# The first sixteen modulation chunks: products and row-block sums on VectorE, TensorE sums over the partitions alone

## The chip, the cores and the metric
The kernel runs on one core of a Trainium2 chip. The metric is the device time of one execution in microseconds; lower is better. TensorE is called PE in the profile, VectorE DVE, ScalarE ACT, GpSimd POOL, SyncE SP.

## The reference, cut to what matters
A stack of two transformer-like layers (gated linear attention, attention, convolution, feed-forward) is run on a context and a latent sequence of 256 tokens each, 1024 channels wide, and then a second stack of two layers. Everything is float32. Each layer of the first stack begins with a modulation, of which the first layer's first two parts, shift and scale, are needed before any other matrix product:

```python
silu_c = jax.nn.silu(c)            # (1, 1024), the latent's condition
silu_cc = jax.nn.silu(c_ctx)       # (1024,), the context's
mod = (silu_c @ w_ada[l] + b_ada[l])[:, None, :]       # w_ada[l]: 1024 x 6144
sh1, sc1, g1, sh2, sc2, g2 = jnp.split(mod, 6, axis=-1)
mod_c = jnp.split(silu_cc @ w_ada[l][:, :n_cm * D_MODEL] + ..., n_cm)
hc = _layernorm(xc) * (1.0 + mod_c[1]) + mod_c[0]
```

Shift and scale are columns 0 to 2047 of `w_ada[0]`: 16 chunks of 128 columns, each a sum over 1024 rows (8 row blocks of 128), for two condition vectors (streams).

## The kernel before, in words
Activations lie with channels on the partitions: `X[:, c, t]` is channel block c of 8, token t. Each large product is made of three float32r products (high and low parts of weights and activations). The weights come as one stream of tiles through three slots: SP loads a slot, ScalarE rounds it to the high part (L1040, `split_to`), GpSimd subtracts for the low part (L1009), PE multiplies (L472 to L474; L485 to L489 for the first two chunks of a pass).

The head of the program goes as follows. SP (L409 to L422) issues loads in this order on one queue: the condition vectors `cvec`, the context tokens `X`, `const1`, then sixteen loads of 512 KB, one per modulation chunk, into `a_first` (eleven places in the arena, five in `s_f32`, L288), then the first three tiles of the stream, then the parameters (`vec1`, the low-rank weights `wglr`, the masks as float32 in `stage`, the latent tokens). ScalarE applies SiLU to `cvec` (L1351), splits the three stream tiles (L1353), then serves the layer norm: a table load, squares (L1077), and the root of the variance (L1069). PE sums the tokens over the channels (L564), then the squares (L573), by products with the constant matrix `mean1024`. VectorE centres the tokens (`centre`, L1588) and turns the root into 1/std (`inverse`, L1577 to L1580).

Then comes `first_modulation` on each engine, between `inverse` and the scaling of the centred tokens. PE runs `ada` for the 16 chunks of `FIRST_UNITS` (L509 to L523): for each of 8 row blocks a product with the 128 x 128 weight block as the stationary operand and the two columns of `cvec` as the moving one, accumulated in a PSUM bank. ScalarE copies each chunk's two columns from PSUM to `mod` (L1234). VectorE casts the masks to bytes (L1908), adds the bias in two instructions of 8 chunks (L1769, `modulation`), waits for ScalarE's rounding of `wglr` (L1361) and subtracts for its low part (L1913). After that VectorE scales each chunk of tokens (`scale_chunk`, L1592), ScalarE adds the shift and rounds it (L1084), VectorE makes its low part (L1599), and PE begins with the dense products, which wait for both.

Order between engines is by semaphores that only count up. `lin_done` and `lin_evac` count PSUM banks filled and emptied, four banks in turn. `step` on VectorE makes it wait for its own last instruction. The other 80 modulation chunks (`ADA_LATER`) are loaded one at a time by ScalarE into `a_raw` and run in gaps later on; their work isn't changed. `gate_buf` and `y_buf` are buffers of 512 columns each that later stages use for sigmoids and branch outputs; they are unused in the head.

Of the kernel before, what the change touches and what calls it, by code (L numbers as in the profile page):

```python
# [28 lines left out]
P = 128  # L29
D = 1024  # L30
KC = D // P
S = 256
# [97 lines left out]
FIRST_UNITS = [("ada", (0, c)) for c in range(ADA_FIRST)]  # L130

# [64 lines left out]
def program(nc, stream, ada_in, xt_in, cvec_in, vec1_in, vec2_in, glr_in, a2_in, const1_in, const2_in, small2_in, mask_in, out):  # L196
# [5 lines left out]
    with ExitStack() as ctx:  # L202
# [85 lines left out]
        a_first = [view(arena, 4 * S * c, KC, P) for c in (*range(10), 12)]  # L288
        a_first += [s_f32[:, 4 * c:4 * c + 4, :].rearrange("p a (b m) -> p (a b) m", m=P) for c in range(5)]
# [25 lines left out]

        def c1(name):
            at, n = CONST1[name]
            return const1[:, at:at + n]
# [9 lines left out]
        def v2(l, name, c=0):  # L328
# [7 lines left out]
        first_landed = [sem(f"first_landed{i}") for i in range(4)]  # L336
# [5 lines left out]
                 "params", "c_landed", "ada_landed", "x_landed", "b2_landed", "stored",  # L342
# [65 lines left out]
        def _(sp):  # L408
# [4 lines left out]
            for c in range(ADA_FIRST):  # L413
                sp.dma_start(a_first[c], ada_in[c]).then_inc(first_landed[c // 4], 16)
# [21 lines left out]
        def _(pe):  # L436
# [70 lines left out]
            ada_done = {}  # L507

            def ada(unit):  # L509

                k0 = len(ada_done)
                ada_done[unit] = k0
                if k0 < ADA_FIRST:
                    w = a_first[k0]
                    if k0 % 4 == 0:
                        pe.wait_ge(first_landed[k0 // 4], 4 * 16)
                else:
                    w = a_raw
                    pe.wait_ge(sems["ada_landed"], 16 * (k0 - ADA_FIRST + 1))
                o = bank()  # L520
                for k in range(KC):
                    mm = pe.matmul(o[:, 0:2], w[:, k, :], cvec[:, k, :], start=k == 0, stop=k == KC - 1)  # L522
                done(mm)  # L523

# [249 lines left out]
            for turn, (l, s) in enumerate(PASSES):  # L774
# [249 lines left out]
        def _(act):  # L1024
# [208 lines left out]
            def ada(l, c):  # L1233
                moved(act.activation(mod[:, l, c, :], arrived(0)[:, 0:2], ACT.Copy))  # L1234
                ada_moved.append((l, c))
                following = len(ada_moved) - ADA_FIRST
                if 0 < following < len(ADA_LATER):
                    act.dma_start(a_raw[:, :, :], ada_in[ADA_FIRST + following]).then_inc(sems["ada_landed"], 16)
# [1112 lines left out]
```

## Time and profile before

| | us |
|---|---|
| median of 3 runs (lowest to highest) | 3371.79 (3366.3 to 3377.26) |
| the profiled execution, its own time | 3385.26 |
| its span in the profile | 3383.5 |
| mean granted TensorE clock | 0.928 of full |
| PE busy | 3011.1 (89%) |
| DVE busy | 2166.1 (64%) |
| POOL busy | 2127.6 (63%) |
| ACT busy | 1521.1 (45%) |

The profiled execution is one run with the recorder on; its own time stands beside its span, and both lie above the median of the three runs. Durations are read from it. Lines such as L522 are lines of the kernel before. PEclk is the clock that TensorE was granted, as a share of 2.4 GHz. A float32 product on PE is recorded as two matmuls and two weight loads.

### The profile page before, as it was taken

What the parts mean: (1) busy time and instruction counts of PE and PEld (TensorE: products, weight loads), DVE (VectorE), ACT (ScalarE), POOL (GpSimd) and SP (SyncE); (2) the same over time, 40 slices, a digit from 0 to 9 for tenths busy, and PEclk for the clock granted to TensorE, in tenths of its full rate; (3) what the DMA queues carried; (4) which work ended last, traced back from release to release, by engine and by line L of the source; (5) the groups of instructions that cost most, each with busy time, mean ns of one, the idle gap of its engine ahead of it and who ended that gap; (6) DMA issues with size and microseconds to landing.
All of it is one profiled execution on the core that took longest, in us unless ns stands there. A gap on an engine that the chain in (4) does not pass through costs nothing.

```text
span 3383.5 us, 59733 instructions
## 1 busy us (share of the span) xinstructions
PE 3011.1 (89%) x21908; PEld 2837.3 (84%) x21908; DVE 2166.1 (64%) x2956; ACT 1521.1 (45%) x3134; POOL 2127.6 (63%) x1906
## 2 busy tenths in 40 slices
PE   6879988889987999889988889888899989998998
PEld 5879887889987977889987789678799869996998
DVE  0776475677695569567654965785676566646655
ACT  1443434344554433435555534334444445554544
POOL 0784545648887453656865964537487637873677
PEclk6889988999998989989999999889899989998999
DMA  5334333435433333334532443223455314542454
GB/s 200 104 127 138 113 112 103 144 116 177 165 125 126 118 106 116 122 113 148 175 131 81 132 144 119 94 82 110 143 179 171 119 46 160 175 156 67 134 169 166
DMA packets 121589, 441.84 MB, mean 131 GB/s; under 512 B 13552, under 2 KB 15600, under 8 KB 120992
## 3 DMA queue, kind: packets, MB, share of 16 engines
q1 hardware_dynamic: 109568, 393.35, 34.8%
q10 hardware_dynamic: 11808, 45.42, 3.9%
q8 instruction: 162, 2.65, 0.3%
q14 instruction: 51, 0.42, 0.0%
HBM read 437.67 MB, written 1.05 MB: 130 GB/s over the span
## 4 chain that ended last, share of the span: by engine, by line
issue 36%; POOL 33%; PE 21%; DVE 7%; ACT 2%; POOLq 1%; DMA 0%; DVEq 0%; ACTq 0%; SPq 0%
POOL w_lo L1009 33%; PE lin L472 5%; PE lin L473 5%; PE lin L474 5%; DVE arena L1702 4%; PE aux L710 2%; PE lin L522 1%; ACT w_hi L1040 1%; DVE s_lo L1640 1%; PE aux L598 1%; POOLq L1011 0%; ACT arena L1200 0%; PE lin L730 0%; POOLq L1007 0%; DVE small L1716 0%
## 5 line engine op out<-in xcount | busy, mean ns | idle before, releaser
L1009 POOL TENSOR_TENSOR w_lo<-w_raw,w_hi 128x256 fp32r<-128x256 f32 (+1 forms) x1902 | 2127.4, 1147 | 1249.5 <-ACT w_hi L1040 1246.7
L472 PE MATMUL lin<-h_hi,w_hi 128*128 128x256 f32 x3584 | 1043.0, 291 | 53.0 <-POOL w_lo L1009 33.6
L473 PE MATMUL lin<-h_lo,w_hi 128*128 128x256 f32 x3584 | 1025.3, 286 | 0.0
L474 PE MATMUL lin<-h_hi,w_lo 128*128 128x256 f32 x3584 | 1024.2, 286 | 0.0
L1040 ACT ACTIVATE w_hi<-w_raw 128x512 fp32r<-128x512 f32 x1446 | 827.8, 623 | 159.6 <-PE lin L472 106.7
L472 PEld LDWEIGHTS lin<-h_hi,w_hi 128*128 128x128 f32 x3584 | 700.0, 195 | 71.2 <-issue 40.2
L473 PEld LDWEIGHTS lin<-h_lo,w_hi 128*128 128x128 f32 x3584 | 699.9, 195 | 0.4
L474 PEld LDWEIGHTS lin<-h_hi,w_lo 128*128 128x128 f32 x3584 | 699.0, 195 | 0.0
L1702 DVE SCALAR_TENSOR_TENSOR arena<-arena,vec 128x256 f32<-128x256 f32 x720 | 453.2, 701 | 0.1
L472 PE MATMUL lin<-s_hi,w_hi 128*128 128x256 f32 x1392 | 415.7, 299 | 31.1 <-DVE s_lo L1640 26.3
L473 PE MATMUL lin<-s_lo,w_hi 128*128 128x256 f32 x1392 | 404.0, 290 | 0.0
L474 PE MATMUL lin<-s_hi,w_lo 128*128 128x256 f32 x1392 | 403.2, 290 | 0.0
L472 PEld LDWEIGHTS lin<-s_hi,w_hi 128*128 128x128 f32 x1392 | 277.1, 199 | 46.5 <-DVE s_lo L1640 34.3
L473 PEld LDWEIGHTS lin<-s_lo,w_hi 128*128 128x128 f32 x1392 | 278.1, 200 | 1.1 <-issue 0.8
L474 PEld LDWEIGHTS lin<-s_hi,w_lo 128*128 128x128 f32 x1392 | 277.5, 199 | 0.0
L1678 DVE TENSOR_TENSOR y_buf<-gate_buf,y_buf 128x256 f32<-128x256 f32 x110 | 147.2, 1338 | 182.7 <-ACT y_buf L1173 182.7
L1640 DVE TENSOR_TENSOR s_lo<-y_buf,s_hi 128x256 fp32r<-128x256 f32 x110 | 232.6, 2115 | 3.8
L1577 DVE RECIPROCAL rstd<-std 128x256 f32<-128x256 f32 (+1 forms) x34 | 59.5, 1749 | 247.9 <-ACT std L1069 247.9
L1657 DVE SCALAR_TENSOR_TENSOR X<-X,gate_buf 128x256 f32<-128x256 f32 x72 | 76.7, 1066 | 149.2 <-ACT gate_buf L1181 70.1
L522 PEld LDWEIGHTS lin<-cvec,a_raw 128*128 128x128 f32 x1280 | 160.1, 202 | 14.3 <-DMA a_raw<-in_ada 11.9
L522 PE MATMUL lin<-cvec,a_raw 128*128 128x2 f32 x1280 | 157.5, 254 | 9.9 <-DMA a_raw<-in_ada 9.9
L500 PE MATMUL lin<-w_hi,h_hi 128*128 128x256 f32 x320 | 97.4, 304 | 54.2 <-POOL w_lo L1009 53.9
(251 smaller groups left out, 4384.7 us busy)
## 6 DMA issues: line engine op xcount, KB each, us to landing
w_raw<-in_stream SPq DMA_DIRECT2D x723, 512.0 KB, 3.3
a_raw<-in_ada ACTq DMA_DIRECT2D x80, 512.0 KB, 3.4
arena<-in_ada SPq DMA_DIRECT2D x11, 512.0 KB, 12.5
s_f<-in_ada SPq DMA_DIRECT2D x5, 512.0 KB, 15.8
X<-in_tokens SPq DMA_DIRECT2D x2, 1024.0 KB, 12.1
arena<-in_const ACTq DMA_DIRECT2D x1, 1856.0 KB, 9.5
arena<-in_small ACTq DMA_DIRECT2D x1, 1536.0 KB, 12.9
out<-arena SPq DMA_DIRECT2D x1, 1024.0 KB, 3.9
```

Source lines behind the costliest of these rows:

```text
L472: used(pe.matmul(o, whi, hi[:, k, :], start=k == 0, stop=False), first)
L473: pe.matmul(o, whi, lo[:, k, :], start=False, stop=False)
L474: mm = pe.matmul(o, wlo, hi[:, k, :], start=False, stop=k == kcs - 1)
L500: mm = pe.matmul(o[:, 0:2 * P], xhi, whi, start=k == 0, stop=False)
L522: mm = pe.matmul(o[:, 0:2], w[:, k, :], cvec[:, k, :], start=k == 0, stop=k == KC - 1)
L710: mm = pe.matmul(pair[kt][:, h * P:(h + 1) * P], part, part, start=True, stop=True)
L1009: ins = pool.tensor_tensor(w_lo[:, slot, part], w_raw[:, slot, part], w_hi[:, slot, part].bitcast(F32), ALU.subtract)
L1040: act.activation(w_hi[:, slot, part], w_raw[:, slot, part], ACT.Copy).then_inc(sems["hi_ready"], 1)
L1640: dve.tensor_tensor(lo, y, hi.bitcast(F32), ALU.subtract).then_inc(sems[name], 1)
L1657: dve.scalar_tensor_tensor(x[:, c, :], x[:, c, :], alpha, gate_buf[:, c % 2, :], ALU.mult, ALU.add).then_inc(sems["r_ready"], 1)
L1678: step(dve.tensor_tensor(y, gate_buf[:, c % 2, :], y, ALU.mult))
L1702: dve.scalar_tensor_tensor(CV[:, c, :], YP[:, c, tap:tap + S], v1(l, "conv_w", c * TAPS + tap), CV[:, c, :], ALU.mult, ALU.add).then_inc(s ...
```

## The change
The weights of the first 16 chunks are laid out in device memory as one array `first` of 128 partitions x 8 row blocks x 2048 columns, and loaded in five groups of 4, 4, 4, 2 and 2 chunks. For each group and each of the two streams VectorE multiplies the eight row blocks by the condition's values (a column of scalars per row block) and adds them up, into `gate_buf` for the context stream and `y_buf` for the latent one: one product and seven multiply-adds per stream. PE then takes each chunk's 128 x 128 part of such a sum as the stationary operand and one column of `mean1024` (1/1024) as the moving one, so that it sums over the partitions; ScalarE multiplies by 1024 while it copies the group's columns to `mod`. VectorE waits for that copy before it begins the next group. The mask cast moves behind the groups and the bias.

```diff
+FIRST_GROUPS = [(0, 4), (4, 4), (8, 4), (12, 2), (14, 2)]
...
-        a_first = [view(arena, 4 * S * c, KC, P) for c in (*range(10), 12)]
-        a_first += [s_f32[:, 4 * c:4 * c + 4, :].rearrange("p a (b m) -> p (a b) m", m=P) for c in range(5)]
+        a_first = [view(arena, 0, KC, 4 * P), view(arena, 16 * S, KC, 4 * P),
+                   s_f32[:, 0:16, :].rearrange("p (k a) m -> p k (a m)", k=KC),
+                   view(arena, 32 * S, KC, 2 * P), view(arena, 48 * S, KC, 2 * P)]
...
+        first_parts = [t[:, :, :].rearrange("p a b -> p (a b)") for t in (gate_buf, y_buf)]
...
 SP:
-            for c in range(ADA_FIRST):
-                sp.dma_start(a_first[c], ada_in[c]).then_inc(first_landed[c // 4], 16)
+            for g, (c, k) in enumerate(FIRST_GROUPS):
+                sp.dma_start(a_first[g], first_in[:, :, c * P:(c + k) * P]).then_inc(first_landed[g], 16)
...
 PE:
+            def first_sums():
+                for g, (_, k) in enumerate(FIRST_GROUPS):
+                    pe.wait_ge(sems["part_ready"], 2 * g + 2)
+                    o = bank()
+                    for c in range(k):
+                        for st, part in enumerate(first_parts):
+                            at_col = 2 * c + st
+                            mm = pe.matmul(o[:, at_col:at_col + 1], part[:, c * P:(c + 1) * P], c1("mean1024")[:, 0:1],
+                                           start=True, stop=True)
+                    done(mm)
...
                         layernorm(x)
+                        first_sums()
                         pe.wait_ge(sems["c_ready"], at.up("c_ready"))
-                        for u in FIRST_UNITS:
-                            unit(l, s, u)
...
 ACT:
             def first_modulation():
-                for u in FIRST_UNITS:
-                    unit(0, u)
+                for c, k in FIRST_GROUPS:
+                    moved(act.activation(mod[:, 0, c:c + k, :], arrived(0)[:, 0:2 * k].rearrange("p (c s) -> p c s", s=2), ACT.Copy,
+                                         scale=float(D)))
...
 DVE:
             def first_modulation():
+                dve.wait_ge(sems["c_ready"], 1)
+                for g, (c, k) in enumerate(FIRST_GROUPS):
+                    dve.wait_ge(first_landed[g], 16)
+                    if g:
+                        dve.wait_ge(sems["lin_evac"], n.at("lin_evac"))
+                    for kc in range(KC):
+                        for st, part in enumerate(first_parts):
+                            w, by = a_first[g][:, kc, :], cvec[:, kc, st:st + 1]
+                            if kc == 0:
+                                ins = dve.tensor_scalar(part[:, 0:k * P], w, by, None, ALU.mult)
+                            else:
+                                dve.wait_ge(sems["dve_step"], n.at("dve_step") - (1 if kc < KC - 1 or st == 0 else 0))
+                                ins = dve.scalar_tensor_tensor(part[:, 0:k * P], w, by, part[:, 0:k * P], ALU.mult, ALU.add)
+                            if kc < KC - 1:
+                                ins.then_inc(sems["dve_step"], 1)
+                                n.up("dve_step")
+                            else:
+                                ins.then_inc(sems["part_ready"], 1)
+                    n.up("lin_evac")
+                    pending.extend((0, c + i, n.at("lin_evac")) for i in range(k))
                 dve.wait_ge(sems["params"], PARAMS)
+                modulation()
                 step(dve.tensor_copy(masks[:, :, :], stage[:, :, :]))
-                for u in FIRST_UNITS:
-                    unit(0, u)
-                modulation()
```

The rest of the diff keeps the count of the other 80 chunks' loads, which no longer follow 16 others in the same array.

## Rows read from the trace of the kernel before

**Rows 1.** The page: busy time of the engines; the loads of X.
```profile
PE 3011.1 (89%) x21908; PEld 2837.3 (84%) x21908; DVE 2166.1 (64%) x2956; ACT 1521.1 (45%) x3134; POOL 2127.6 (63%) x1906
...
X<-in_tokens SPq DMA_DIRECT2D x2, 1024.0 KB, 12.1
```

**Rows 2.** Who waited for whom, 0 to 105 us: total, times, longest (us).
```profile
ACT mod L1234 <- PE lin L522: 49.5, 16, 3.2
DVE mod L1769 <- ACT mod L1234: 47.8, 2, 27.1
```

**Rows 3.** Timeline of the head: start, length (us), engine, line, operation, count, idle before.
```profile
16.90 2.48 DVE L1588 TENSOR_TENSOR arena<-X,aux 128x512 f32<-128x512 f32 x4 [16.90 <-PE aux L564]
...
35.16 1.15 ACT L1040 ACTIVATE w_hi<-w_raw 128x512 fp32r<-128x512 f32 x2 [0.15 <-DMA w_raw<-in_stream]
...
38.40 5.97 PE L573 MATMUL aux<-M,const 128*128 128x256 f32 x16 [21.54 <-ACT M L1077]
...
44.21 35.53 PE L522 MATMUL lin<-cvec,arena 128*128 128x2 f32 x176
...
44.82 1.75 DVE L1577 RECIPROCAL rstd<-std 128x256 f32<-128x256 f32 x1 [25.45 <-ACT std L1069]
...
46.61 0.42 DVE L1578 SCALAR_TENSOR_TENSOR tmp<-aux,rstd 128x256 f32<-128x256 f32 x1
...
47.53 0.42 DVE L1580 SCALAR_TENSOR_TENSOR rstd<-tmp,rstd 128x256 f32<-128x256 f32 x1
47.99 1.16 DVE L1908 CAST masks<-arena 128x1920 uint8<-128x1920 f32 x1
...
79.60 17.21 PE L522 MATMUL lin<-cvec,s_f 128*128 128x2 f32 x80
...
96.84 0.17 ACT L1234 ACTIVATE mod<-lin 128x2 f32<-128x2 f32 x1 [3.24 <-PE lin L522]
...
97.12 0.18 DVE L1769 SCALAR_TENSOR_TENSOR mod<-mod,vec 128x16 f32<-128x16 f32 x1 [27.13 <-ACT mod L1234]
97.85 0.96 DVE L1913 TENSOR_TENSOR wglr_lo<-arena,wglr_hi 128x768 fp32r<-128x768 f32 x1 [0.56 <-ACT wglr_hi L1361]
98.72 0.87 DVE L1592 SCALAR_TENSOR_TENSOR arena<-arena,mod,rstd 128x256 f32<-128x256 f32 x2
```

**Rows 4.** Stretches of the head: length, busy time per engine, PEclk, DMA share, GB/s.
```profile
6.00:8.00 2.00, 0.00 (x0) 0.00 (x0) 0.00 (x0) 0.00 (x0) 0.00 (x0) 1.00 1.07 421
20.00:24.00 4.00, 0.00 (x0) 0.00 (x0) 0.00 (x0) 0.00 (x0) 0.00 (x0) 0.50 1.03 410
38.00:42.00 4.00, 3.60 (x9) 2.89 (x10) 0.00 (x0) 1.90 (x4) 3.55 (x6) 0.50 1.02 347
48.00:97.00 49.00, 48.81 (x229) 48.72 (x229) 1.32 (x2) 2.57 (x16) 0.00 (x0) 0.50 0.00 1
100.00:104.00 4.00, 3.45 (x16) 3.48 (x17) 4.00 (x11) 2.32 (x6) 0.00 (x0) 0.50 0.00 0
104.00:108.00 4.00, 4.00 (x34) 4.00 (x34) 1.76 (x6) 0.96 (x3) 0.00 (x0) 0.95 0.02 4
```

**Rows 5.** Timeline, VectorE and PE at the start of the dense work.
```profile
99.78 0.48 DVE L1599 SCALAR_TENSOR_TENSOR h_lo<-arena,mod,h_hi 128x256 fp32r<-128x256 f32 x1 [0.18 <-ACT h_hi L1084]
...
100.52 0.29 PEld L485 LDWEIGHTS lin<-h_hi,w_hi 128*128 128x128 f32 x1 [3.80 <-issue]
...
100.97 0.48 DVE L1592 SCALAR_TENSOR_TENSOR arena<-arena,mod,rstd 128x256 f32<-128x256 f32 x1
```

**Rows 6.** Lengths of one instruction (ns, min/median/max): L1807 and L1588.
```profile
L1807 DVE SCALAR_TENSOR_TENSOR arena<-arena x8: 1212/1451/1687, 204.8 to 1950.7; 128x1024 f32<-128x1024 f32 x8
...
L1588 DVE TENSOR_TENSOR arena<-X,aux x52: 673/681/689, 16.9 to 2648.2; 128x512 f32<-128x512 f32 x52
```

**Rows 7.** L522: lengths in the head (ns), and one chunk later in the kernel.
```profile
L522 PEld LDWEIGHTS lin<-cvec,s_f x80: 333/333/333, 79.5 to 96.4; 128*128 128x128 f32 x80
...
236.69 1.84 PE L522 MATMUL lin<-cvec,a_raw 128*128 128x2 f32 x16
```

More of the change, by code:

```diff
@@ L193, with program @@
 assert sorted(u[1] for u in FIRST_UNITS + ADA_LATER) == [(l, c) for l in range(DEPTH) for c in range(ADA_CHUNKS)]
-def program(nc, stream, ada_in, xt_in, cvec_in, vec1_in, vec2_in, glr_in, a2_in, const1_in, const2_in, small2_in, mask_in, out):
+def program(nc, stream, first_in, ada_in, xt_in, cvec_in, vec1_in, vec2_in, glr_in, a2_in, const1_in, const2_in, small2_in, mask_in, out):
     F32 = mybir.dt.float32
@@ L335, in program @@
         landed = [sem(f"landed{i}") for i in range(SLOTS)]
-        first_landed = [sem(f"first_landed{i}") for i in range(4)]
+        first_landed = [sem(f"first_landed{i}") for i in range(len(FIRST_GROUPS))]
         NAMES = ("hi_ready",
@@ L505, in token_major @@
                             done(mm)
-            ada_done = {}
+            ada_done = []
             def ada(unit):
[L511 to L519, printed above, removed]
+                ada_done.append(unit)
+                pe.wait_ge(sems["ada_landed"], 16 * len(ada_done))
                 o = bank()
                 for k in range(KC):
-                    mm = pe.matmul(o[:, 0:2], w[:, k, :], cvec[:, k, :], start=k == 0, stop=k == KC - 1)
+                    mm = pe.matmul(o[:, 0:2], a_raw[:, k, :], cvec[:, k, :], start=k == 0, stop=k == KC - 1)
                 done(mm)
+            def first_sums():
[8 more added lines that the diff above has]
+                    done(mm)
             def unit(l, s, u):
@@ L1235, in ada @@
                 ada_moved.append((l, c))
-                following = len(ada_moved) - ADA_FIRST
-                if 0 < following < len(ADA_LATER):
-                    act.dma_start(a_raw[:, :, :], ada_in[ADA_FIRST + following]).then_inc(sems["ada_landed"], 16)
+                if len(ada_moved) < len(ADA_LATER):
+                    act.dma_start(a_raw[:, :, :], ada_in[len(ada_moved)]).then_inc(sems["ada_landed"], 16)
             def unit(l, u):
@@ L2187, in ada_tiles @@
     both = [tiles(w["w_ada"]).reshape(ADA_CHUNKS, KC, P, P).transpose(0, 2, 1, 3) for w in layers]
-    return np.stack([both[l][c] for _, (l, c) in FIRST_UNITS + ADA_LATER])
+    return np.stack([both[l][c] for _, (l, c) in ADA_LATER])
 def half_tiles(gate, up, down):
@@ L2331 @@
         "stream": np.concatenate(stream).reshape(LOADS, TILES, P, P).transpose(0, 2, 1, 3).reshape(LOADS, P, TILES * P),
+        "first": layers[0]["w_ada"][:, 0:ADA_FIRST * P].reshape(KC, P, ADA_FIRST * P).transpose(1, 0, 2),
         "ada": ada_tiles(layers),
```

4 lines of the change are left out of this document (2 added, 2 removed).

## Prediction, written before the changed kernel was run

> **What bounds the kernel now.** The page first: TensorE (PE) is busy for 89% of the span, but that is an average over stages, and the change touches only the head of the program [rows 1]. So the next view is who waited for whom in the head: ScalarE waits 49.5 us for the modulation's matmuls (L522), and VectorE 47.8 us for ScalarE behind them; no wait is longer in total [rows 2]. The timeline of that stretch gives the order [rows 3]. The weight loads land; ScalarE, which waited for the last of them, splits until 36.31; PE sums ScalarE's squares from 38.40 to 44.37; after ScalarE's root VectorE makes 1/std, 44.82 to 47.95. Beside that PE begins the 16 chunks at 44.21 and ends them at 96.81. Then ScalarE moves the last chunk (96.84 to 97.01), VectorE adds the bias (97.12 to 97.30), splits the low-rank weights (97.85) and starts to scale chunks at 98.72; PE's dense work begins at 100.52 [rows 5]. POOL is idle, all slots being full [rows 4]. Nothing runs in the gap that could absorb a delay, so a microsecond here is one at the end.
>
> **What goes.** 16 chunks of 8 products, each recorded as two matmuls: 256 records from 44.21 to 96.81, 52.6 us, 0.2055 each on average, 0.2135 in the steady part at 3.416 per chunk (ScalarE waits 3.24 and works 0.17 for each) [rows 3]. The granted clock there is 0.50, so this is the 1.2 GHz level [rows 4]. PE could start them at 44.2, beside VectorE's 1/std; the new work stands behind 1/std in VectorE's own order and starts at 47.99, where the mask cast stands now. So to gain anything it would have to be done in under 49.1 us (97.12 less 47.99).
>
> **What comes: VectorE's sums.** Per group 8 row blocks by 2 streams, 16 instructions: 2 plain products and 14 multiply-adds. Three groups are 512 columns wide, two 256: 42 and 28 multiply-adds, 6 and 4 products. No row shows a multiply-add of 512 columns. The nearest in kind are L1592 and L1599, a column of scalars as here, 256 columns: 0.48 long, but started every 0.40 (99.78 to 100.97 is three steps) with a semaphore wait between them [rows 5]. The new ones wait for the instruction before the last, so they can follow one another as closely. For the width: 1024 columns take 1.212 at best [rows 6] against 0.42 for 256 (L1578 [rows 3]), 1.03 ns a column; 256 more add 0.265, so 0.66 apart. Bounds: 0.60 (four subtractions of 512 columns, 0.681 each, in 2.48 [rows 3, 6]) and 0.73 (each waits for the one before: L1578 to L1580 are two steps in 0.92 at 256 columns, plus 0.265 each). The products take one tensor: the cast's 1.16 for 1920 columns is 0.60 ns a column, so I take 0.40 and 0.27. Sum: 42 x 0.66 + 6 x 0.40 + 28 x 0.40 + 4 x 0.27 = 27.7 + 2.4 + 11.2 + 1.1 = **42.4 us**. With 0.60 and 0.36 it is 38.8, with 0.73 and 0.46 it is 47.1. POOL is idle throughout, so nothing contends with VectorE for SBUF but PE's reads, which I cost at nothing; L1807's span from 1.212 to 1.687 [rows 6] shows what company can cost, and the high bound stands for it.
>
> The rows give 0.40 for 256 columns. The Trainium skill, "VectorE: DVE Perf Modes", section "Side-by-side: where the cycles go for N=2048 bf16", counts columns + 8 + about 150 cycles at 0.96 GHz, an estimate of 0.70 for 512 and 0.43 for 256. By that the sum would be about 45 us and the time 3 us longer; the rows at 256 speak for less, and I keep them.
>
> **The new wait.** There is one pair of partial sums (gate_buf, y_buf). From the second group on, VectorE waits until ScalarE has moved the previous group, so each group is a serial round trip: VectorE's last end is 0.09 behind its issue pace; PE's start behind VectorE 0.26 (L1599 ends at 100.26, PE's weight load starts at 100.52 [rows 5]); the matmuls; ScalarE 0.03 later, 0.17 long; VectorE 0.11 later [rows 3]. A matmul with one column instead of two still loads 128 x 128 weights (0.333 long each, overlapped [rows 7]); I take nothing for the column saved, so 8 products for a group of four chunks cost as much as one chunk did: 16 x 0.2135 = 3.42, plus 0.23 to fill and drain the first and last. That is 4.3 per wide group, 2.6 per narrow one: 3 x 4.3 + 2 x 2.6 = **18.1 us**, of which nothing is covered, because VectorE has no other work and the next group's first product writes the same buffer. PE's clock: idle from 16.9 it was granted 0.50, and it stayed at 0.50 through narrow matmuls [rows 4], so the bursts run slow. At full clock they would be worth half: 16 records in 1.84 [rows 7].
>
> **The end of the head.** Start 47.99 + 42.4 + 18.1 = 108.5 where 97.12 stands now: +11.4. Both bias additions of 0.18 now stand at the end; one was hidden before (L1769 waited twice, 20.7 and 27.1 [rows 2]): +0.2. The mask cast of 1.16 was hidden under PE and now lies behind them, in front of the split of the low-rank weights, but it covers the 0.56 that VectorE waited for ScalarE there [rows 3]: net +0.7. Sum **+12.3 us**.
>
> **The loads.** 8.39 MB as before. Five issues instead of 16 take SP out of the way sooner, worth nothing: the engines are full at 410 GB/s from 6 us on, the queue is served in order and the stream's tiles stand behind the same bytes. The runs shrink from 4 KB to 2 KB and 1 KB. X has 1 KB runs (256 columns), and the stretch that carries it shows 421 [rows 1, 4]; so I take nothing for it. The other bound is the 347 GB/s of 38 to 42 us: 24.2 us instead of 20.5, +3.7. All have landed before the stream's tiles, by 36, long before VectorE asks at 48.
>
> After the head all is as before, moved; the banks' order shifts by 11 chunks, nobody waits for that. The granted clock rises about 4 us after dense work starts, as now (0.50 in 100 to 104 us, 0.95 in 104 to 108 [rows 4]); at half clock those 4 us hold 2 us of work, so a rise that comes at once or twice as late is worth 2 us either way.
>
> **Rivals.** (a) *Full clock or quicker hand-over in the bursts:* 1.8 less three times, 0.9 twice, 7.2 off: +5.1, 3377, no measurable change. For it: PE was at 1.00 while idle at 6 to 8 us [rows 4]. Against: 0.50 in the idle stretch of 20 to 24 us. 0.15. The low bound for VectorE (-3.6) gives +8.7, which also can't be told from zero. (b) *VectorE serial, or the loads late:* 47.1 instead of 42.4 is +17.0; late loads move the root and all behind it by 3.7, +16.0; both, +20.7, 3392. For it: a wait stands before every instruction and the rows' runs are new. 0.15. (c) *Not slower:* VectorE forms two columns a cycle in the multiply-add as in the cast. Then 48 x 0.40 + 32 x 0.27 = 27.8 replaces 42.4: -14.6, so -2.3, 3369. It decides at about 0.40 apart for 512 columns. Against: the multiply-adds of 256 and 1024 columns differ by 1.03 ns a column, where the cast shows 0.60. 0.04. (d) *The change doesn't do what it says:* PE isn't relieved, since a narrow matmul costs its weight load. That is in the forecast: PE still does 32 products of 128, in a place where VectorE stands still for them.
>
> **Numbers.** A measurement of this kernel tells 0.3%, 10.1 us, from no change. The profiled execution took 3385.3 (span 3383.5) against a median of 3371.8 (3366.3 to 3377.3); the sum is a difference and goes on either: 3397.6 profiled, 3384.1 for the median. Forecast 0.66; its own band of +8 to +16 lies for about a quarter on the near side of +10.1. Slower: 0.66 x 0.74 + 0.15 = 0.64. Faster: 0.03, half of (c) and some disturbance. Same: 0.33. The range goes from (a) to (b) with 2 us for the median's scatter: 3375 to 3393.
>
> **What would show it.** VectorE busy for some 42 us in about 48 to 111 us, in five blocks of about 10.2 and 6.2 with four gaps of 4.3 and 2.6; PE in five bursts, three of 16 records and two of 8, 0.21 apart, clock 0.50; modulation at 108.5, mask cast behind it, PE's first dense work at 112.8. Wrong if the 512-column instructions start under 0.60 apart, the gaps are under 3 us, or 1/std ends elsewhere than at 48.

## The result, and the profile after

| | us |
|---|---|
| kernel before, median of 4 runs | 3374.53 (3366.3 to 3382.57) |
| changed kernel, median of 4 runs | 3404.72 (3402.06 to 3407.11) |
| ratio | 1.0089, 95% interval 1.0062 to 1.0116 |
| forecast | 3384.1, range 3375 to 3393: +12.3 |
| profiled execution of the changed kernel | 3405.85 (before: 3385.26) |
| its span | 3404.1 (before: 3383.5) |
| its mean granted clock | 0.925 (before: 0.928) |

Slower, as forecast, but by 30 us instead of 12. The two spans are 20.6 us apart.

The page of the changed kernel, the rows that answer to [rows 1]: PE works 34 us less (the 128 products that go took 52.6, 32 new ones come), VectorE 38 us more.

```profile
PE 2977.3 (87%) x21716; PEld 2803.1 (82%) x21716; DVE 2204.3 (65%) x3036; ACT 1518.5 (45%) x3123; POOL 2122.4 (62%) x1906
...
arena<-in_first SPq DMA_DIRECT2D x2, 2048.0 KB, 16.4
```

Who waited for whom, 0 to 115 us (total, times, longest), against [rows 2]: PE now waits for VectorE, ScalarE for PE, and VectorE four times for ScalarE, 14.1 us in total.

```profile
ACT mod L1366 <- PE lin L530: 61.5, 5, 17.0
...
PE lin L530 <- DVE y_buf L1927: 48.1, 5, 13.8
...
DVE gate_buf L1924 <- ACT mod L1366: 14.1, 4, 4.0
```

Timeline of its head, against [rows 3, 5], first VectorE, then PE and ScalarE.

```profile
47.75 1.75 DVE L1585 RECIPROCAL rstd<-std 128x256 f32<-128x256 f32 x1 [28.12 <-ACT std L1077]
...
50.91 0.49 DVE L1924 TENSOR_SCALAR gate_buf<-arena,cvec 128x512 f32<-128x512 f32 x1
51.32 0.48 DVE L1924 TENSOR_SCALAR y_buf<-arena,cvec 128x512 f32<-128x512 f32 x1
51.71 0.75 DVE L1927 SCALAR_TENSOR_TENSOR gate_buf<-arena,cvec,gate_buf 128x512 f32<-128x512 f32 x1
52.38 0.75 DVE L1927 SCALAR_TENSOR_TENSOR y_buf<-arena,cvec,y_buf 128x512 f32<-128x512 f32 x1
53.04 0.75 DVE L1927 SCALAR_TENSOR_TENSOR gate_buf<-arena,cvec,gate_buf 128x512 f32<-128x512 f32 x1
...
65.02 0.49 DVE L1924 TENSOR_SCALAR gate_buf<-arena,cvec 128x512 f32<-128x512 f32 x1 [3.95 <-ACT mod L1366]
...
93.95 0.48 DVE L1927 SCALAR_TENSOR_TENSOR gate_buf<-arena,cvec,gate_buf 128x256 f32<-128x256 f32 x1
94.34 0.48 DVE L1927 SCALAR_TENSOR_TENSOR y_buf<-arena,cvec,y_buf 128x256 f32<-128x256 f32 x1
...
110.20 0.17 DVE L1777 SCALAR_TENSOR_TENSOR mod<-mod,vec 128x16 f32<-128x16 f32 x1 [2.15 <-ACT mod L1366]
110.41 1.16 DVE L1937 CAST masks<-arena 128x1920 uint8<-128x1920 f32 x1
111.60 0.96 DVE L1939 TENSOR_TENSOR wglr_lo<-arena,wglr_hi 128x768 fp32r<-128x768 f32 x1
112.48 0.88 DVE L1600 SCALAR_TENSOR_TENSOR arena<-arena,mod,rstd 128x256 f32<-128x256 f32 x2
```

```profile
40.54 6.76 PE L582 MATMUL aux<-M,const 128*128 128x256 f32 x16 [23.43 <-ACT M L1085]
61.13 0.59 PE L530 MATMUL lin<-const,gate_buf 128*128 128x1 f32 x2 [13.83 <-DVE y_buf L1927]
...
114.28 0.55 PE L489 MATMUL lin<-h_hi,w_hi 128*128 128x256 f32 x1 [4.38 <-DVE h_lo L1607]
```

```profile
34.73 3.72 ACT L1048 ACTIVATE w_hi<-w_raw 128x512 fp32r<-128x512 f32 x6 [31.96 <-DMA w_raw<-in_stream]
...
64.74 0.18 ACT L1366 ACTIVATE mod<-lin 128x8 f32<-128x8 f32 x1 [17.02 <-PE lin L530]
```

The multiply-adds of 512 columns start 0.66 apart, those of 256 0.39 to 0.40. VectorE stands idle for 3.95 before a group of four. The first token chunk is scaled at 112.48 instead of 98.72: the head is 13.8 us longer. That leaves 6.8 of the trace's 20.6 us for the 3290 us behind the head.

Stretches of the head (columns as in [rows 4]; the last is GB/s). The loads are slower than the 410 of [rows 4] from 20 us on:

```profile
20.00:24.00 4.00, 0.00 (x0) 0.00 (x0) 0.00 (x0) 0.00 (x0) 0.00 (x0) 0.50 1.05 387
24.00:28.00 4.00, 0.00 (x0) 0.00 (x0) 0.00 (x0) 0.00 (x0) 0.00 (x0) 0.50 1.07 371
28.00:32.00 4.00, 0.00 (x0) 0.00 (x0) 0.00 (x0) 0.00 (x0) 0.00 (x0) 0.50 1.11 352
```

### The profile page after: what moved, and what is told of

The parts are those of the page before. It is cut to its first block, busy times and chain, and to the rows that moved or that the text cites. A ratio compares the mean times of both kernels' runs of the same rounds, so it can differ in the third digit from the quotient of the medians.

```text
span 3404.1 us, 59409 instructions
## 1 busy us (share of the span) xinstructions
PE 2977.3 (87%) x21716; PEld 2803.1 (82%) x21716; DVE 2204.3 (65%) x3036; ACT 1518.5 (45%) x3123; POOL 2122.4 (62%) x1906
## 3 DMA queue, kind: packets, MB, share of 16 engines
q8 instruction: 169, 2.77, 0.4%
## 4 chain that ended last, share of the span: by engine, by line
issue 30%; PE 29%; POOL 28%; DVE 10%; ACT 2%; POOLq 1%; DMA 1%; DVEq 0%; ACTq 0%; SPq 0%
POOL w_lo L1017 28%; PE lin L476 7%; PE lin L477 6%; PE lin L478 6%; DVE arena L1710 5%; PE aux L719 2%; PE lin L519 2%; DVE s_lo L1648 1%; PE aux L607 1%; ACT w_hi L1048 1%; PE lin L739 1%; PE aux L647 1%; ACT arena L1208 1%; DVE small L1724 1%; DVE s_hi L1647 0%
## 5 line engine op out<-in xcount | busy, mean ns | idle before, releaser
L1648 DVE TENSOR_TENSOR s_lo<-y_buf,s_hi 128x256 fp32r<-128x256 f32 x110 | 221.9, 2017 | 4.0 <-DVE s_hi L1647 0.3
L519 PEld LDWEIGHTS lin<-cvec,a_raw 128*128 128x128 f32 x1280 | 158.3, 200 | 13.6 <-DMA a_raw<-in_ada 11.1
L504 PE MATMUL lin<-w_hi,h_hi 128*128 128x256 f32 x320 | 96.8, 303 | 53.1 <-POOL w_lo L1017 52.6
## 6 DMA issues: line engine op xcount, KB each, us to landing
X<-in_tokens SPq DMA_DIRECT2D x2, 1024.0 KB, 11.1
s_f<-in_first SPq DMA_DIRECT2D x1, 2048.0 KB, 20.9
```

The lines of the kernel that those rows point to most:

```text
L504: mm = pe.matmul(o[:, 0:2 * P], xhi, whi, start=k == 0, stop=False)
L519: mm = pe.matmul(o[:, 0:2], a_raw[:, k, :], cvec[:, k, :], start=k == 0, stop=k == KC - 1)
L1648: dve.tensor_tensor(lo, y, hi.bitcast(F32), ALU.subtract).then_inc(sems[name], 1)
```

## The experiments

Where a text below speaks of microseconds "to the median", it is the ratio less one, times the median of the kernel before in the same comparison. "Head" is the start of the first scaled token chunk against the 98.72 of the first trace of before.

Two readings stood against each other at first: that a microsecond of head costs more than one at the end, and that the change also costs something behind the head, where its code does nothing.

### Is it the head, and which part of it?

**after_again** is the changed kernel once more.

> The changed kernel once more, beside the kernel before in five rounds. Its trace showed the head 13.8 us longer (the first scaling of tokens at 112.48 instead of 98.72), its span 20.6 and the medians 30. If the head is all there is, the ratio settles at +14 us (1.004) and the rest was scatter of the few runs. If something behind the head costs too, it stays at +25 to +35 us.

1.0085 (1.0059 to 1.0112), +28.7 us, head +12.7: the result stands.

**before_delay4** lets PE do the first four chunks twice, so that only the head is longer:

```diff
-                for k in range(KC):
-                    mm = pe.matmul(o[:, 0:2], w[:, k, :], cvec[:, k, :], start=k == 0, stop=k == KC - 1)
+                for _ in range(2 if k0 < 4 else 1):
+                    for k in range(KC):
+                        mm = pe.matmul(o[:, 0:2], w[:, k, :], cvec[:, k, :], start=k == 0, stop=k == KC - 1)
```

> The kernel before, with the eight products of the first four chunks done twice on TensorE: the head is 4 x 3.41 = 13.7 us longer and nothing else differs. Theory 'whatever comes late by 13.7 us also loses time later' (the granted clock's levels fall otherwise on the stages): +25 to +35 us, like the changed kernel. Rival 'a delay costs itself': +13.7, and what the changed kernel loses beyond that belongs to the changed kernel itself.

Head +10.6 (the first repeats still ran at full clock), time 1.0059 (1.0037 to 1.0082), +19.9 us. Expected were +13.7 for the head, and +25 to +35 or +13.7 for the time. So a delay of the head with none of VectorE's new work in it also seems to cost more than itself, which spoke for something behind the head. The repeats also put 128 instructions more ahead of PE's later code; 2.3 us are of the kind found below, and the sum of +12.9 lies at the lower end of the interval.

**after_contiguous** lays each group out so that a partition's part is one run of 16 or 8 KB:

```diff
-                sp.dma_start(a_first[g], first_in[:, :, c * P:(c + k) * P]).then_inc(first_landed[g], 16)
+                sp.dma_start(a_first[g], first_in[:, c * KC * P:(c + k) * KC * P].rearrange("p (a b) -> p a b", a=KC)).then_inc(first_landed[g], 16)
```

> The changed kernel with each group's weights contiguous per partition in device memory (16 or 8 KB runs instead of 2 and 1 KB). Theory 'the short runs slow the loads': the DMA rate from 20 to 32 us returns from 352 to 387 GB/s to 410, the stream's first tiles land 2.1 us sooner and 1/std ends near 48 instead of 50.88: 3 us less than the changed kernel. Rival 'the larger loads or the order of issue cost it': nothing changes.

The loads run at 428 and 416 GB/s where the changed kernel had 387 and 371:

```profile
20.00:24.00 4.00, 0.00 (x0) 0.00 (x0) 0.00 (x0) 0.00 (x0) 0.00 (x0) 0.50 1.01 428
24.00:28.00 4.00, 0.00 (x0) 0.00 (x0) 0.00 (x0) 0.00 (x0) 0.00 (x0) 0.50 1.00 416
```

The head is 3.4 us shorter than in the first trace of the changed kernel, 2.3 shorter than in the second. The time, 1.0077 (1.0051 to 1.0102), is 2.7 us lower than that of after_again; the intervals don't part the two.

**after_two_pairs** adds a second pair of partial sums (in `M`, which is free there), so that VectorE waits for ScalarE only two groups back:

```diff
-                    if g:
-                        dve.wait_ge(sems["lin_evac"], n.at("lin_evac"))
+                    if g > 1:
+                        dve.wait_ge(sems["lin_evac"], n.at("lin_evac") - 1)
...
-                        for st, part in enumerate(first_parts):
+                        for st, part in enumerate(first_parts[g % 2]):
```

> The changed kernel with a second pair of partial sums, so that VectorE waits for the group before the last. The four gaps on VectorE (three of 3.95, one of 2.24 us, 14.1 in all) vanish, PE's bursts lie under VectorE's sums: the first scaling moves from 112.5 to about 98.4, the time falls by 14 us if a microsecond of the head is one at the end; by more or less if the stages behind it answer to where they fall.

The groups follow one another without a gap, 10.07 apart instead of 14.1:

```profile
50.08 0.49 DVE L1925 TENSOR_SCALAR gate_buf<-arena,cvec 128x512 f32<-128x512 f32 x1
50.48 0.48 DVE L1925 TENSOR_SCALAR y_buf<-arena,cvec 128x512 f32<-128x512 f32 x1
60.15 0.88 DVE L1925 TENSOR_SCALAR M<-arena,cvec 128x512 f32<-128x512 f32 x2
70.22 0.48 DVE L1925 TENSOR_SCALAR gate_buf<-s_f,cvec 128x512 f32<-128x512 f32 x1
```

The head is 15.5 us shorter than the changed kernel's and 1.7 shorter than before's. Yet the time is 1.0033 (1.0018 to 1.0048), +11.1 us. With both edits, **two_pairs_contiguous**:

> The changed kernel with two pairs of partial sums and contiguous groups. By the parts measured so far the first scaling comes at about 94.5 (97.02 with two pairs, less 2.5 for the loads), 4 us sooner than in the kernel before. If each microsecond of the head is one at the end: -4 us against the kernel before. If what these kernels lose behind the head stays (two pairs alone: head 1.7 us shorter, time 10 us longer): +6 to +8.

Head -5.5, time 1.0012 (0.9991 to 1.0032), +4.0 us. A shorter head and no gain: by the middle values some 10 us are lost elsewhere, whatever the head does.

### Two versions that shorten the head

**before_copy** is the kernel before, unchanged, **pe_six_early** has PE do six chunks, which have landed, between mean and variance, where it stands idle, in one bank with one move to `mod`:

```diff
-                        layernorm(x)
+                        for k in range(KC):
+                            mean_chunk(x, k)
...
-                        for u in FIRST_UNITS:
+                        first_together(TOGETHER)
+                        variance(M)
+                        for u in FIRST_UNITS[TOGETHER:]:
```

> The kernel before, unchanged, as a kernel of its own: what five rounds say where nothing differs, and a second trace of it. Scatter theory: ratio within 0.998 to 1.002, and the times of the marks behind the head differ from the first trace of the kernel before by several microseconds either way, as the granted clock's levels fall. Rival: the kernel before repeats itself within 2 us from the head on, and the 12 us that the changed kernel loses behind its head are its own.

> The kernel before, with the first six chunks on TensorE between the sums of the tokens and of their squares, where it is idle from 16.9 to 38.4 us; VectorE does nothing of it. Six chunks less behind the squares at 3.41 us each: the first scaling at about 98.7 - 20.5 + up to 4 (chunks that start late because their weights land at 18 to 22 us push the squares' sums back) = 78 to 82, time -17 to -20 us. If the end doesn't follow the head: less than half of that.

before_copy: 0.9988 (0.9969 to 1.0008). Its span is 3358.8, 24.7 us under the first trace of the same kernel, with the same head (98.41). Its mean granted clock is 0.934 against 0.928, and from 98 to 380 us 0.97 against 0.93: the same code meets the lower level in other places and for other lengths. So single traces aren't compared by their ends below.

pe_six_early: head -22.5 (expected -17 to -21), time 0.9929 (0.9904 to 0.9954), -23.9 us. That agrees with a microsecond of head being one at the end, within some 8 us either way.

**vector_early** keeps VectorE's sums, but for 12 chunks in three groups and ahead of 1/std, where VectorE stands idle, with two pairs of sums; PE does the other four chunks directly while it waits. In vector_early the array `first` is packed in the order of the groups and read by chunk number, so that chunks 4 to 15 of `mod` are exchanged among each other, at the same cost. **vector_early_mended** has them in place.

```diff
+                        for k in range(KC):
+                            mean_chunk(x, k)
+                        first_direct()
+                        first_sum(0)
+                        variance(M)
+                        first_sum(1)
+                        first_sum(2)
```

> VectorE forms its sums where it is idle, between centring and 1/std (19.6 to 47.8 us in the traces), for 12 chunks in three groups with two pairs of buffers; TensorE does the other four chunks directly while it is idle before the squares. VectorE: 3 x 10.2 from about 19.6, then 1/std 3.2; TensorE: 4 x 3.41 from about 21, one burst, the squares' sums, two bursts. First scaling at 57 to 60 instead of 98.7: -39 to -42 us if the end follows the head. The theory behind it: the place on VectorE's own order, behind 1/std, is what made the change worthless, not the price of its instructions.

> As vector_early, with the groups' weights laid out in the order in which they are read; the first one computed with chunks exchanged, at the same cost. TensorE's dense work started at 60.3 instead of 100.5 there, and the time fell by 31 us in the median of six runs. The same again: -31 to -40 us. GpSimd took 27.6 us for the first three tiles' low parts beside VectorE's sums instead of 8.25, so the kernel can't gain more than up to about 59.8 us.

Head -41.4 and -41.7; time 0.9887 (0.9858 to 0.9916) and 0.9911 (0.9888 to 0.9933), -38.1 and -30.1 us. Both beat both kernels. They ran in two different comparisons, the intervals overlap, and by the medians the two are 31.5 and 30.1 us under the kernel before, so the 8 us between the ratios are no difference that is shown. POOL's twelve low parts, which now begin beside VectorE's sums, take 27.23 us; in pe_six_early, with VectorE idle, they take 8.23. First vector_early_mended, then pe_six_early:

```profile
32.22 27.23 POOL L1032 TENSOR_TENSOR w_lo<-w_raw,w_hi 128x256 fp32r<-128x256 f32 x12 [31.77 <-ACT w_hi L1063]
```

```profile
34.22 8.23 POOL L1023 TENSOR_TENSOR w_lo<-w_raw,w_hi 128x256 fp32r<-128x256 f32 x12 [33.76 <-ACT w_hi L1054]
```

The lengths of the twelve in vector_early_mended (ns, minimum, median, maximum) show that one of them, the first, takes 17.36 us: it starts at 32.2 and ends at 49.5, when VectorE's sums are over. The other eleven stand beside what VectorE does next, and there VectorE is held up as well: of its three like steps of 1/std the first takes 0.42 us, the others 0.77 and 0.83.

```profile
L1032 POOL TENSOR_TENSOR w_lo<-w_raw,w_hi x12: 717/902/17357, 32.2 to 58.5; 128x256 fp32r<-128x256 f32 x12
```

```profile
50.69 0.42 DVE L1601 SCALAR_TENSOR_TENSOR tmp<-aux,rstd 128x256 f32<-128x256 f32 x1
51.15 0.77 DVE L1602 SCALAR_TENSOR_TENSOR tmp<-tmp,rstd 128x256 f32<-128x256 f32 x1
51.95 0.83 DVE L1603 SCALAR_TENSOR_TENSOR rstd<-tmp,rstd 128x256 f32<-128x256 f32 x1
```

### What is lost behind the head: PE's loop

PE runs the feed-forward stage as a loop of two turns (`pe.Fori(0, 2)`, L664 before, L673 changed), five times in a pass through the program. All other PE code is straight. The first hint was that the stage around 1640 us took 228.7 us in some kernels and 232 to 233 in others, the one around 2930 us 243 and 248 to 250, whatever the head did, and that the kernels parted by how many PE instructions their head had. The next three kernels change that number and as little else as possible: idle products of two columns into an unused bank, while PE waits anyway.

```diff
+                        for k in range(KC):
+                            mean_chunk(x, k)
+                        for _ in range(32):
+                            pe.matmul(aux[3][:, 0:2], c1("mean1024"), const1[:, 0:2], start=True, stop=True)
+                        variance(M)
```

A product is recorded as four PE instructions, so this is +128; 32 more products before the tokens land make +256.

> The kernel before with 32 two-column products of constants on TensorE while it is idle between the sums of the tokens and of their squares (17 to 38 us): 128 more TensorE instructions, head unchanged (first scaling at 98.7). The traces so far part into two families behind the head: stages that take 228.6 and 242.5 us in the kernels before, with six early chunks and with VectorE early, and 233.2 and 248 to 250 (or 242.4) in the kernel before with delay and the changed kernel's; each kernel keeps its value. TensorE's instructions in the head differ by 0, -2 and -288 in the first family and by +128 and -384 in the second, that is by about 0 or about 128 modulo 256, and instructions are loaded in pieces of 16 KB (queue 8). Theory 'place of the code': this kernel joins the second family, 228.6 becomes 233 and it is 5 to 12 us slower with an unchanged head. Rival 'being late costs more than the delay' or 'the new work on VectorE disturbs later stages': no change, within 3 us.

> As before_plus_128 and 32 more products with 16 columns of weights before the tokens land: 256 more TensorE instructions, head unchanged. Theory 'place of the code' with a period of 16 KB: first family again, 228.6 us in that stage, no change against the kernel before. Rival 'any added instructions cost': slower than before_plus_128.

> The changed kernel with the 32 idle products: its TensorE instructions then are 258 fewer than in the kernel before instead of 386. Head as in the changed kernel (first scaling at 111 to 112.5). Theory 'place of the code': the stage of 233.2 us returns to 228.6, and the time is the kernel before's plus the head, +13 to +15 us instead of +27. Rivals: +25 to +30 as before.

before_plus_128: 1.0011 (0.9999 to 1.0023), +3.7 us; before_plus_256: 1.0004 (0.9989 to 1.0018), +1.4 us. By time the two decide nothing: expected for the first were 5 to 12 us, or less than 3. But the stage near 1640 us went to 233.2 in the first and stayed at 228.7 in the second, as the theory said. after_plus_128: 1.0027 (1.0013 to 1.0042), +9.1 us with a head of +11.7, and the stage at 228.6. Idle work on PE seemed to make the changed kernel faster. It had not run beside the changed kernel yet, so four kernels went side by side: the changed kernel, and it with 16 products (+64), 32 (+128) and 64 (+256).

> The changed kernel, unaltered, beside the three that follow. Both theories: 1.0085 of the kernel before, +28 us, first scaling of a token chunk at about 111, VectorE's 1/std to 1/std stage near 1530 to 1760 us 4 us above the kernel before's 228.6 us, the one near 2790 to 3040 us 6 us above its 243.

> The changed kernel with 16 idle products of two columns on PE between mean and variance (64 PE instructions more instead of 128). Theory A (what counts is the place of PE's later code, by PE's instructions in the head against those of the kernel before, repeating every 256): 320 fewer than before, which is 64 short of a full repeat, a place not yet seen; it says only that the time lies between +9 us and +28 us, nearer the lower end if a jump's target just has to miss the last part of a piece. Theory B (the gain of the 32 products was something else of theirs, such as busy time in front of the variance, or chance): half of their gain, +19 us (1.0056).

> The changed kernel with 32 idle products (128 instructions), side by side with the changed kernel for the first time. Theory A: +9 us (1.0027), 15 to 19 us under the changed kernel of the same call, stages near 2790 us back at 243. Theory B, chance of the chip or the hour: no more than 5 us under it.

> As the one before, with 32 more products before the tokens land (256 PE instructions more; 128 fewer than the kernel before). Theory A: the place is again that of the changed kernel, so +25 us or more (1.0075 to 1.009), the late stages 4 and 6 us long again, the head as in the changed kernel or up to 1 us later. Theory B (more idle products in the head make the time shorter, or the first 32 did whatever they did): +9 us or less.

| | head | ratio (95%) | us to the median |
|---|---|---|---|
| after_third | +12.6 | 1.0075 (1.0049 to 1.0100) | +25.3 |
| after_plus_64 | +12.7 | 1.0040 (1.0025 to 1.0056) | +13.5 |
| after_plus_128_again | +11.6 | 1.0049 (1.0031 to 1.0066) | +16.5 |
| after_plus_256 | +13.9 | 1.0077 (1.0047 to 1.0107) | +26.0 |

Theory B (the idle products themselves help) is out: twice as many undo the gain. The mean of the 13 runs of the first and last is 10.2 us above that of the 12 between (95%: about 4.5 to 16). That 128 brings a little less than 64 is within the scatter. The size expected for 128, 15 to 19 us under the changed kernel, was missed: it is 8.8.

The traces show what happens. In after_third, at the fourth loop, the branch back to the second turn takes 3651 ns (ns, minimum, median and maximum of the one instruction, then its start):

```profile
L673 PEldq COMPARE_BRANCH  x1: 3651/3651/3651, 2916.2 to 2916.2; - x1
```

The matmuls around it in the same trace: PE stops for 5.21 us while it waits for nothing that the profile shows, and goes on at 0.41 a matmul instead of 0.28.

```profile
2918.11 0.28 PE L478 MATMUL lin<-s_hi,w_lo 128*128 128x256 f32 x1
2923.60 0.58 PE L489 MATMUL lin<-h_hi,w_hi 128*128 128x256 f32 x1 [5.21 <-issue]
2923.97 0.42 PE L492 MATMUL lin<-h_lo,w_hi 128*128 128x256 f32 x1
2924.19 0.41 PE L493 MATMUL lin<-h_hi,w_lo 128*128 128x256 f32 x1
```

The stretches behind the stop: the granted clock (third from the end) is 0.50, the 1.2 GHz level, for four microseconds and 0.84 over the next four.

```profile
2924.00:2928.00 4.00, 4.00 (x20) 4.00 (x20) 0.00 (x0) 0.00 (x0) 0.00 (x0) 0.50 0.29 115
2928.00:2932.00 4.00, 4.00 (x31) 4.00 (x30) 0.00 (x0) 0.23 (x1) 0.00 (x0) 0.84 0.00 0
```

And the queue that loads instructions, 2900 to 2960 us (packets, MB, share of 16 engines):

```profile
q8 instruction: 6, 0.10, 0.7%
```

The same in after_plus_64, whose code is the same but for 16 idle products 2800 us earlier. The branch, the matmuls, and the queue over the same 60 us:

```profile
L673 PEldq COMPARE_BRANCH  x1: 236/236/236, 2915.0 to 2915.0; - x1
```

```profile
2916.94 0.28 PE L478 MATMUL lin<-s_hi,w_lo 128*128 128x256 f32 x1
2918.14 0.38 PE L489 MATMUL lin<-h_hi,w_hi 128*128 128x256 f32 x1 [0.93 <-POOL w_lo L1021]
2918.36 0.28 PE L492 MATMUL lin<-h_lo,w_hi 128*128 128x256 f32 x1
```

```profile
q8 instruction: 1, 0.02, 0.1%
```

A piece is 16 KB (2.77 MB in 169 packets by the page of the profile of the changed kernel). Over the stretch from the branch at 2916.2 to the end of the second turn at 3021.3, after_third moves nine of them, the first while PE stands at the branch; over the same turn in after_plus_64 none moves. Nine in after_third:

```profile
q8 instruction: 9, 0.15, 0.6%
```

That holds without exception: the 18 traces have 90 such turns, 46 with a slow branch and nine pieces each, 44 with a quick one and none. A turn is 1661 recorded PE instructions, 6.5 pieces of 256. So a slow branch is one behind which PE's code is loaded again. In the kernel before the second loop's branch takes 214 ns, in the changed kernel 3351:

```profile
L664 PEldq COMPARE_BRANCH  x1: 214/214/214, 1628.5 to 1628.5; - x1
```

```profile
L673 PEldq COMPARE_BRANCH  x1: 3351/3351/3351, 1642.5 to 1642.5; - x1
```

Read so for each of the five loops (the branch back in us, and from it to the end of the second turn, which is 98.2 to 98.5 us where the branch is quick):

| kernel | PE's weight loads and matmuls in the head against before | 1 | 2 | 3 | 4 | 5 | sum of the turns |
|---|---|---|---|---|---|---|---|
| before | 0 | 0.24 / 98.3 | 0.21 / 98.3 | 3.39 / 100.6 | 0.22 / 98.2 | 3.94 / 101.9 | 497.3 |
| before_copy | 0 | 0.24 / 98.3 | 0.21 / 98.3 | 3.64 / 100.8 | 0.22 / 98.2 | 3.38 / 101.0 | 496.6 |
| changed | -384 | 4.34 / 101.5 | 3.35 / 102.8 | 0.23 / 98.3 | 3.33 / 103.5 | 0.22 / 98.2 | 504.3 |
| after_third | -384 | 4.44 / 101.6 | 3.73 / 103.5 | 0.23 / 98.3 | 3.65 / 105.2 | 0.22 / 98.2 | 506.8 |
| after_plus_256 | -128 | 4.43 / 101.6 | 3.69 / 103.5 | 0.23 / 98.3 | 3.37 / 103.8 | 0.22 / 98.2 | 505.4 |
| after_plus_64 | -320 | 3.93 / 101.0 | 0.23 / 98.3 | 4.45 / 101.6 | 0.24 / 98.5 | 3.66 / 99.3 | 498.7 |
| after_plus_128_again | -256 | 0.24 / 98.3 | 0.21 / 98.3 | 3.74 / 100.9 | 0.22 / 98.5 | 3.46 / 100.8 | 496.8 |
| before_plus_128 | +128 | 4.54 / 101.6 | 3.35 / 103.0 | 0.23 / 98.3 | 0.22 / 98.2 | 0.21 / 98.2 | 499.3 |

A branch costs either 0.2 or 3.3 to 4.8 us (the 4.8 in before_delay4). Which ones are slow goes by the place of the code and comes back after 256 instructions: -256 is as 0, -128 as -384. The other ten traces fit: before_plus_256 (+256), after_plus_128 (-256) and pe_six_early (0) have the slow loops 3 and 5 of the kernel before; after_again, after_contiguous, after_two_pairs and two_pairs_contiguous (-384) have 1, 2 and 4; before_delay4 (+128) has 1 and 2; both versions with VectorE early (-288) have 1, 3 and 5. Only +128 doesn't match -128 and -384, in loop 4. There the column is too coarse: with the sequencer's own instructions the changed kernel has 386 fewer ahead of its first loop, not 384, so +128 and -384 are two instructions off a full repeat.

Counting every recorded PE instruction ahead of a branch back, the body of each earlier loop once, gives one rule for all 90: the slow branches stand at places 166 to 255 and 0 to 28 of 256, the quick ones at 29 to 159. Loop 4 stands at 27 in the changed kernel and at 29 in before_plus_128. This edge is narrow, since the counts of one kernel differ by up to four between traces, and the rule is read off these 18 traces, not derived.

The kernel before has two slow branches, the changed kernel three, with longer turns behind them. In the trace of the changed kernel that is 504.3 less 497.3, +7.0 us. The branches of the other engines take at most 0.07 us in every trace, so VectorE's and ScalarE's changed counts cost nothing of this kind.

"Runtime: NRT & Kernel Launch" of the Trainium skill, section "🔬 Instruction fetch mechanics", says that instructions come in blocks of 16 KB, 256 of them, and that a taken branch whose target isn't in the window held forces a fetch of the target's page before work goes on. By that rule the slow branches are such fetches, and the traces agree: pieces of 16 KB, a period of 256, and nine pieces behind each slow branch against none behind a quick one.

### The sum for every kernel

Head and loops, each from the kernel's one trace against the first trace of before, beside the measured time:

| kernel | head | loops | sum | measured (95%) |
|---|---|---|---|---|
| changed | +13.8 | +7.0 | +20.8 | +30.0 (20.9 to 39.1) |
| after_again | +12.7 | +6.9 | +19.6 | +28.7 (19.9 to 37.8) |
| after_third | +12.6 | +9.5 | +22.1 | +25.3 (16.5 to 33.7) |
| after_plus_256 | +13.9 | +8.1 | +22.0 | +26.0 (15.9 to 36.1) |
| after_contiguous | +10.4 | +9.0 | +19.4 | +26.0 (17.2 to 34.4) |
| after_plus_64 | +12.7 | +1.4 | +14.1 | +13.5 (8.4 to 18.9) |
| after_plus_128 | +11.7 | -0.9 | +10.8 | +9.1 (4.4 to 14.2) |
| after_plus_128_again | +11.6 | -0.5 | +11.1 | +16.5 (10.5 to 22.3) |
| after_two_pairs | -1.7 | +10.9 | +9.2 | +11.1 (6.1 to 16.2) |
| two_pairs_contiguous | -5.5 | +8.6 | +3.1 | +4.0 (-3.0 to 10.8) |
| before_delay4 | +10.6 | +2.3 | +12.9 | +19.9 (12.5 to 27.7) |
| before_plus_128 | -0.3 | +2.0 | +1.7 | +3.7 (-0.3 to 7.8) |
| before_plus_256 | +1.0 | +1.4 | +2.4 | +1.4 (-3.7 to 6.1) |
| before_copy | -0.3 | -0.7 | -1.0 | -4.0 (-10.4 to 2.7) |
| pe_six_early | -22.5 | -1.2 | -23.7 | -23.9 (-32.3 to -15.5) |
| vector_early | -41.4 | +2.5 | -38.9 | -38.1 (-47.9 to -28.3) |
| vector_early_mended | -41.7 | +2.4 | -39.3 | -30.1 (-37.8 to -22.6) |

Two terms carry the results from -38 to +30 us. Fourteen of the seventeen sums lie in the interval measured, which is 8 to 20 us wide; that of vector_early_mended is 1.5 us outside, those of the changed kernel and after_again 0.1 and 0.3. What is left of the span without the head and the five turns lies between 2764 and 2793 us in the 18 traces. Its mean is 2780.6 in the seven with the slow loops of the changed kernel and 2782.0 in the other eleven, so the traces show no third place where the change costs.

## Why the prediction was wrong, point by point

**VectorE's sums: right.** Multiply-adds of 512 columns are 0.66 apart, of 256 0.40, as taken; a wide group takes 10.07 (the spacing of the groups in after_two_pairs), as the sum had it (14 x 0.66 + 2 x 0.40 = 10.04). The 0.70 that comes from the count of the Trainium skill, "VectorE: DVE Perf Modes", section "Side-by-side: where the cycles go for N=2048 bf16", is an estimate that lies between the recorded length, 0.75, and the spacing. Rival (c) is out.

**The new wait: right, slightly high.** A wide group begins 14.11 behind the one before it (50.91 to 65.02), so the trip costs 4.04 against 4.3; the narrow one costs about 2.3 against 2.6. That makes 3 x 4.04 + 2 x 2.3 = 16.7 instead of 18.1. PE's burst ran at 0.427 a product, twice the 0.2135 a record that [rows 3] shows at the granted clock of 0.50, so rival (a) is out. Of rival (b) the late loads came, with 2.1 of its 3.7 us; VectorE serial did not. Taking the wait away (after_two_pairs) shortened the head by 15.5, of which 14.1 are VectorE's waits and 0.8 an earlier 1/std.

**The start of the sums: wrong by 2.9.** It was put at 47.99 and came at 50.91. The step that failed is the one on the loads: "X has 1 KB runs, and the stretch that carries it shows 421; so I take nothing for it". With runs of 2 and 1 KB the loads fell to 387, 371 and 352 GB/s, ScalarE's first split moved from 32.59 to 34.73, and contiguous runs gave it back (416 to 428). Its own bound, +3.7, held it. The row was also misread: only 248 of the 1024 packets of X, 0.25 of 0.84 MB, fall in 6 to 8 us. Most of X moved in the two microseconds before, at lower rates, in which the queue was also just starting (kernel before):

```profile
4.00:5.00 1.00, 0.00 (x0) 0.00 (x0) 0.00 (x0) 0.00 (x0) 0.00 (x0) 1.00 0.86 242
5.00:6.00 1.00, 0.00 (x0) 0.00 (x0) 0.00 (x0) 0.00 (x0) 0.00 (x0) 1.00 1.03 340
```

The rest, 0.8 us, is PE's variance at a lower clock: 6.76 us at a mean granted clock of 0.54 against 5.97 at 0.62.

**The end of the head: nearly right, in part by luck.** +12.3 forecast, +13.8 in the trace, +12.7 and +12.6 in two more. The late start of 2.9 is offset by waits 1.4 us cheaper than priced. The +0.2 for a second bias addition didn't come: it ran at 107.88, under the last wait. The +0.7 for the mask cast did.

**"After the head all is as before, moved": this failed,** and it is the largest error of the prediction. The 96 products that the change takes from PE's head are 384 instructions of code. Behind them every later PE instruction has another place, and the branch back is slow in three of five loops instead of two: +7.0 us in the trace, 6.9 to 10.9 in the six other traces with the same slow loops. Side by side, moving the code back by idle products took 10.2 us off. No term of the sum stood for it. With the head's 13.8 the two terms make 20.8. That alone is still at the edge of the range, which ended at +21 for VectorE and loads; the measured +30 lies 9 us further, in what stays open below. That the two traces are 20.6 apart is no proof of the sum: the two traces of the kernel before differ by 23.7 us outside the head and the loops.

**What stays open.** The measured times of the changed kernel lie 3 to 9 us above its sums, that of after_contiguous 7. The same kernel's executions differ by 20 us and more: the 23 of the kernel before that ran beside before_copy go from 3354.3 us, at a mean granted clock of 0.936, to 3384.2 at 0.928. Whether the clock falls worse for the changed kernel wasn't settled; the 3 to 9 us may be this scatter. Why a branch is slow at places 166 to 28 of 256 and not at the others isn't derived.

## What to carry to other kernels

Price a moved or removed instruction also by what its absence shifts: where an engine's long code has a loop, count the instructions ahead of it, look at the branch's duration in the trace of before (0.2 or 3.3 to 4.8 us here), and when a result is off by a few microseconds in stages that weren't touched, try some idle instructions ahead before looking for a cause in the change. A sum moved to an idle engine must also start while that engine is idle: behind 1/std VectorE's sums for 16 chunks made the head 14 us longer, ahead of it those for 12 chunks, with two pairs of sums, contiguous loads and four chunks left to PE, made it 41 us shorter. And a serial hand-over per group through one buffer cost 14 us of waits, which a second buffer took away.

## What the runs showed of the hardware

- **A branch back of PE** takes 0.21 to 0.24 us or 3.3 to 4.8 us, by the place of the code, with a period of 256 instructions. Behind each of 46 slow ones nine pieces of 16 KB are loaded until the turn ends, behind each of 44 quick ones none. A slow one adds 1 to 8 us to the turn; in the case looked at, the granted clock fell to 0.50 behind the stop.
- **POOL beside VectorE:** twelve subtractions of 128x256 took 27.2 us where they began beside VectorE's float32 multiply-adds with a column of scalars, and 8.2 alone. The first of them lasted 17.4 us, until the multiply-adds ended, while VectorE kept its pace of 0.66; behind that VectorE's own instructions of 0.42 took 0.77 and 0.83. The kernel before never has the two together in its head. "SBUF — State Buffer" of the Trainium skill, section "🔬 SBUF: two separate sides", says that a VectorE instruction with two inputs in SBUF and a POOL instruction that reads SBUF take a pair of ports from each other, each for its whole length. The trace agrees: either engine is held up, and VectorE's chain of multiply-adds let POOL in only at its end.
- **Length of the runs:** loads with 2 KB to a partition's run moved 387 GB/s (20 to 24 us), mostly 1 KB runs 352 (28 to 32 us), where 4 KB runs moved 410 and runs of 16 and 8 KB 428 and 416. The distance between the runs in device memory changed with their length, and no run parts the two.
- **A product with one column** takes PE 0.427 us at the granted clock of 0.50, as one with two (2 x 0.2135), so the column saved brings nothing. That the weight load sets the pace is likely, but not shown.
